# Half of the long-cache key products moved from VectorE to POOL, in place, in a two-layer hybrid decoder step

## What is computed

```python
def diff_attention(q, k, v, qpos, lam, lam_init):
    kpos = jnp.arange(k.shape[1], dtype=jnp.int32)
    def blk(qp, qb):
        s = jnp.einsum('bqhmd,bkhmd->bhmqk', qb, k) * (A_QK_DIM ** -0.5)
        p, _, _ = masked_softmax(s, kpos[None, :] <= qp[:, None])
        attn = p[:, :, 0] - lam * p[:, :, 1]
        return jnp.einsum('bhqk,bkhd->bqhd', attn.astype(v.dtype), v)
    o = blockwise(blk, qpos, q)
    return rmsnorm(o) * (1.0 - lam_init)
# for the samples: k = concatenate([cache_a_k[page_table], new key]), 1025 keys of 4 x 2 x 64
```

## Time and profile before

| | |
|---|---|
| median of 3 runs | 826.94 us (823.4 to 831.84) |
| the profiled execution | 828.67 us |
| its span, first to last instruction | 826.9 us |
| mean granted TensorE clock in it | 0.972 of full speed |

### The profile page before, as it was taken

The page is one execution under the profiler, slowest core; times in us unless marked ns, Lnnn a source line. Parts: engine busy times, 40 slices in busy tenths (PEclk is TensorE's granted clock), DMA queues, the critical chain, the costliest instruction groups (busy, mean ns, idle before and its releaser), DMA issues.

```text
span 826.9 us, 12677 instructions
## 1 busy us (share of the span) xinstructions
PE 755.6 (91%) x4874; PEld 404.9 (49%) x4874; DVE 426.0 (52%) x958; ACT 241.2 (29%) x601; POOL 164.6 (20%) x202
## 2 busy tenths in 40 slices
PE   6789999999898899999999998899899799999896
PEld 4456555444454334434454554555464455564543
DVE  2203598999968989645253243323654425421214
ACT  5324333222214101122254323333320233242222
POOL 0332412011330233430101022511131001001000
PEclk9999999999999799999999999999998999999899
DMA  8656668889896678796695394777779967856901
GB/s 287 206 203 220 242 244 320 309 307 376 281 321 209 228 245 299 229 340 247 218 321 183 126 405 166 282 265 273 262 248 386 377 252 284 304 173 258 356 1 54
DMA packets 67829, 213.08 MB, mean 258 GB/s; under 512 B 5056, under 2 KB 28785, under 8 KB 61881
## 3 DMA queue, kind: packets, MB, share of 16 engines
q0 software_dynamic: 20320, 142.55, 47.1%
q1 hardware_dynamic: 47288, 69.62, 24.0%
q10 hardware_dynamic: 160, 0.11, 0.0%
HBM read 206.22 MB, written 64.68 MB: 328 GB/s over the span
## 4 chain that ended last, share of the span: by engine, by line
PE 64%; DVE 17%; DMA 7%; ACT 5%; issue 5%; another core or an unknown queue 1%; POOL 0%; DVEq 0%; ACTq 0%; SPq 0%
PE psum L914 28%; PE psum L980 10%; PE psum L844 7%; PE psum L925 4%; DMA ring<-in_w_in_odd 4%; DVE SA L2334 3%; PE psum L1069 2%; DVE ring L2331 2%; PE psum L895 2%; DMA ring<-in_cache_a_v,index_a 2%; PE psum L1035 2%; PE psum L1320 2%; PE psum L1165 1%; ACT Z L1463 1%
## 5 line engine op out<-in xcount | busy, mean ns | idle before, releaser
L914 PE MATMUL psum<-ring,XB 128*128 128x512 f32 (+3 forms) x760 | 329.3, 587 | 4.1 <-DMA ring<-in_w_in_odd 3.3
L914 PEld LDWEIGHTS psum<-ring,XB 128*128 128x128 f32 x760 | 144.4, 195 | 161.3 <-issue 153.8
L980 PE MATMUL psum<-Z,ring 128*128 128x512 f32 x256 | 119.7, 613 | 2.1 <-issue 1.2
L1892 DVE TENSOR_TENSOR RT<-Z,const 128x128 f32<-128x128 f32 (+6 forms) x43 | 11.5, 267 | 145.1 <-ACT Z L1553 112.5
L980 PEld LDWEIGHTS psum<-Z,ring 128*128 128x128 f32 x256 | 47.2, 193 | 61.9 <-issue 60.8
L1553 ACT ACTIVATE Z<-psum,stat 128x512 f32<-128x512 f32 (+3 forms) x38 | 24.1, 635 | 179.6 <-PE psum L914 172.4
L925 PE MATMUL psum<-ring,XB 128*8 128x128 f32 (+3 forms) x1664 | 49.9, 267 | 4.7 <-issue 3.1
L925 PEld LDWEIGHTS psum<-ring,XB 128*8 128x8 f32 x1664 | 41.6, 89 | 23.0 <-issue 22.0
L1717 ACT ACTIVATE SM<-SM,stat 128x128 f32<-128x128 f32 (+4 forms) x56 | 26.9, 480 | 72.5 <-DVE stat L2081 71.4
L1463 ACT COPY NW<-psum 128x512 f32<-128x512 f32 (+1 forms) x56 | 32.7, 584 | 47.9 <-PE psum L844 41.6
L2164 DVE MAX8 small<-KC 8x8 f32<-8x1025 f32 x32 | 38.9, 1217 | 1.6
(11 more groups left out here) (347 smaller groups left out, 902.0 us busy)
## 6 DMA issues: line engine op xcount, KB each, us to landing
ring<-in_w_in_odd SPq DMA_DIRECT2D x9, 2048.0 KB, 13.2
ring<-in_w_in_even SPq DMA_DIRECT2D x6, 2048.0 KB
ring<-in_cmp_w SPq DMA_DIRECT2D x4, 2048.0 KB
ring<-in_w_in_odd SPq DMA_DIRECT2D x8, 1024.0 KB
out_s_d_k<-in_state_d_k POOLq DMA_DIRECT2D x8, 1022.0 KB
out_s_d_v<-in_state_d_v POOLq DMA_DIRECT2D x8, 1022.0 KB
Z<-in_cmp_w POOLq DMA_DIRECT2D x5, 1024.0 KB, 8.0
ring<-in_state_d_v POOLq DMA_DIRECT2D x5, 1024.0 KB, 7.6
```

Source lines behind the costliest of these rows:

```text
L914: last = mm(out[:, 0:n], xT[:, k, t * 128:(t + 1) * 128], w[:, k * n:(k + 1) * n], start=k == 0, stop=k == KT - 1)
L980: last = mm(out[:, h * 512:(h + 1) * 512], w[:, (r % 16) * CH + h * 128:(r % 16) * CH + h * 128 + 128], rowsT[:, at:at + 512], start=r == ...
```

## The change

For the second half of every entry (half = 1), the product with the query is computed by POOL, in place in the same buffer, and VectorE's `score_a(b, 1)` waits for the semaphore `multiplied` and then only sums. The first halves stay as they were. POOL's product stands in POOL's queue: before an item is issued, POOL multiplies the next entry b if the load `ak{b}_1` is already issued and if the step `score_a(b, 1)` comes at most `POOL_LEAD` = 14 steps of `ORDER` after the step that frees the item's buffer (an item whose former user is no load of POOL counts as free from the start, `default=-1`, and has no product put ahead of it).

```diff
+POOL_LEAD = 14
...
-                kv = ap(slot[:, 0:1], [512, 4], [1, 512])
-                tt(kv, kv, ap(queries[:, 0:1], [0, 4], [1, 512]), mul).then_inc(step, 1)
-                wait_own(step)
+                if half:
+                    eng.wait_ge(sem("multiplied"), b + 1)
+                else:
+                    kv = ap(slot[:, 0:1], [512, 4], [1, 512])
+                    tt(kv, kv, ap(queries[:, 0:1], [0, 4], [1, 512]), mul).then_inc(step, 1)
+                    wait_own(step)
...
+            def multiply(b):
+
+                name = f"ak{b}_1"
+                pool.wait_ge(*arrival[name])
+                if b == 0:
+                    pool.wait_ge(*marks["query_a"])
+                kv = ap(slot_of(name)[:, 0:1], [512, 4], [1, 512])
+                nc.gpsimd.tensor_tensor(kv, kv, ap(queries[:, 0:1], [0, 4], [1, 512]), ALU.mult)\
+                    .then_inc(sem("multiplied"), 1)
+
+
+            issued, multiplied = set(), 0
             for name, queue, parts in items:
                 if queue == "pool":
+                    freed = max([last_use[n] for n in place[name][1] if n in last_use], default=-1)
+                    while multiplied < NB and f"ak{multiplied}_1" in issued \
+                            and step_of["score_a", multiplied, 1] <= freed + POOL_LEAD:
+                        multiply(multiplied)
+                        multiplied += 1
+                    issued.add(name)
                     stream(pool, name, parts)
```

## The result

The changed kernel took a median of 843.81 us (841.71 to 853.13, four runs); the kernel before, on the same chip, 826.4 us (823.4 to 831.84, four runs). The ratio is 1.0225, with a 95% interval from 1.0132 to 1.0318. So the change costs 1.7 to 2.3%, 14 to 19 us by these ratios (17.4 and 12.3 us by the differences of the medians), where 8.0 us were forecast. The profiled executions are 841.71 us (span 839.9) after and 828.67 (span 826.9) before: 13.0 us, and those are the ones that the traces explain.

What follows compares the result with a forecast made beforehand. The prediction took TensorE as the bound, with VectorE's lateness costing at most some 4 us. Added waits of 2.8, 2.2 and 3.0 us summed to 8.0 us, giving a median of 834.9 us, range 825 to 843.

Steps and rivals of the forecast that it cites:

- The price of the multiply: One 128x2048 f32 multiply on POOL: taken as 4.57 us, the upper end, with 2.29 us as the lower.
- The exclusion: POOL's multiplies and VectorE's two-input operations hold each other up, while one-input reductions pass.
- M1 to M3 have room: POOL's multiplies for entries 1 to 3 (M plus entry number): VectorE gains 3 x 2.3 us less what they block.
- Rival 2: Multiplies of entries 1 to 6 each hold VectorE for all 4.57 us: 846.4 us, chance 16%.
- Step B: POOL's multiplies for entries 4 to 6 make VectorE late; 2.2 us reaches TensorE at 226.09 through the softmax.
- Step A: Entry 0's multiply holds a VectorE rope near 83 us, making TensorE's index queries 2.8 us late.
- M4: POOL's multiply for entry 4, queued behind ak6_0, runs 187.1 to 191.7; VectorE's reduction waits, 1.8 us late.
- M5: POOL's multiply for entry 5: waits for VectorE's L2331, runs 198.0 to 202.6, and makes L2055 wait 1.8 us.
- Step C: Entry 7's multiply, behind rows1_2 and four copies, delays TensorE's maxima by 3.0 us, counted from a TensorE event.
- the relief: VectorE loses 18.3 us of multiplies; TensorE's three idle pieces between 100 and 240 us return at most some 4 us.
- Rival 1: No exclusion between POOL and VectorE, multiply price 4.57 us: +1.6, 828.5 us, chance 20%.
- rival 3: A multiply of 2.29 us without exclusion, so VectorE runs ahead: -3.4, 823.5 us, chance 12%.

Runs made afterwards that it cites:

- The kernel with entries 0 to 2: POOL multiplies the second halves of entries 0 to 2 only, VectorE the others, against the kernel before: 814.79 us, ratio 1.0016.
- the second pair: The unaltered changed kernel measured again on another chip against the kernel before: 826.67 us against 814.38, ratio 1.0173.
- the kernel with entries 4 and 5: POOL multiplies the second halves of entries 4 and 5 only, VectorE the others, against the kernel before: 819.84 us, ratio 1.006.

## Why the prediction was wrong, step by step

**The price of the multiply** was right: 4.51 to 4.54 us against 4.57. The Trainium skill's 4.50 us (GPSIMD Engine Reference, Performance versus the Vector engine) is nearer still.

**The exclusion** was right for what it named and named too little. Two-input operations are held (2.94, 5.79 and 4.41 us for 0.29, 0.48 and 2.29). The step that failed is the sentence "M1 to M3 have room": it went through the queue and asked only for two-input operations in the way. M3 met the one-input L2030. Price: 5.1 us of stall and 1.8 us of slower turns behind it, 6.9 us, against nothing. Rival 2 had dismissed the same place with "M1 and M3 meet few of the others". Step B, below, is the other large error and of about the same size.

**Step A**, +2.8, measured 0 (1.0 us ahead at that point). The hold came as told, 2.94 us ending after M0. But TensorE's turn of the index queries began at 83.55, while the rope was held until 85.46, so it was not waiting for the rope. In the earlier trace rows the rope ended 0.48 us before that turn, and the trace named another releaser, which I overrode by nearness. The kernel with entries 0 to 2 bears it out: 8.4 us of holds, and TensorE's distance unchanged over them.

**Step B**, +2.2, measured +9.8 less the 3.4 regained. The wait for M4 came (3.95 us of idle time). The error is what M5 meets. Its readiness was as forecast, 1.8 us after the reduction (201.27 to 203.11). But I had it wait there for the next first-half product and then meet L2055, for 1.8 us, and took L2099 to be over by then. By the records it would have been: it begins at 202.14 and needs 0.48. What failed is the premise that a multiply holds nothing before it begins. L2099, on which TensorE's turn depends directly, was held from 0.97 us before M5's record to its end, 5.3 us more than its own length. M6 and L2335 went nearly as told (4.41 us, a hold of 2.1 against 3.2).

**Step C**, +3.0, measured +2.7; mechanism as written, M7 from 250.09, a wait of 8.12 us for the forecast 8, TensorE idle for 2.55 us. "Counted from a TensorE event" held.

**What was not in the sum.** First, the price of a stall beyond its length: 4.7 us (1.8 and 2.9) in slower turns behind the waits of 5.43 and 7.72 us; the granted clock was 0.50 from 170.0 to 172.6 us and 0.52 from 208 to 214. Second, the relief. "At most some 4 us" became 14 by the ratio, which is why the other two terms, 28 to 32 us by the same ratios, end at 14 to 19. Counting three idle pieces of one trace left out two of the same kind (0.67 and 1.38 us) and what the clock gave back behind them.

**The rivals.** Rival 2, 846.4 us by a hold for every multiply, is closest to the 843.81. That nearness is in part luck, since two of its terms were not right: A cost nothing, and the holds did not cost by their sum (18.0 us) but by the two that a turn of TensorE hung on. Rival 1 (no exclusion) and rival 3 (a short multiply) are excluded by the rows. The forecast's sign was right. Its range ended at 843, seven tenths of the way from 834.9 to rival 2 (the prediction says half way and further), and the first pair left it by 0.8 us; the second pair's 1.0173 would be 841.2 us on the 826.94, inside it. So the number was missed narrowly, because errors of both signs met: A and the relief on one side, entry 3, M5 and the clock on the other.

**What stays open.** L2099's hold begins at 202.14, 0.97 us before M5's record begins; this repeats at 182.62 against 183.62 in the kernel with entries 4 and 5. The load and the copy alone do not do it, as shown above; why the hold starts ahead of the multiply's record was not tested. The 3.6 us (16.6 to 13.0) that come back after 260 us go at least in part with the clock: 2.9 us come back at 778 to 787 us of the kernel before, where its granted clock is 0.52 on the mean, while the changed kernel does the same matmuls at 1.00 (790 to 811 us).

## What to carry to other kernels

Before work is moved to POOL, lay it against VectorE's instructions one by one and sort those by kind, not by number of inputs: reductions, MAX8 and MATCH_REPLACE8 passed beside a multiply, two-input operations and TENSOR_SCALAR on SBUF did not, and the cost is set by the one held operation that the bounding engine waits for. Leave a margin of 1 us ahead of the multiply's recorded start as well. Cut the piece to the length of an instruction that passes and start it by that instruction's predecessor: the same kind of multiply then gave 0.9913 where it had cost 1.02. If an engine has lost work and its busy time has not fallen, look for instructions of unusual length; that is how a hold looks in a profile.

## What the runs showed of the hardware that was not expected

- A fill by POOL, which reads nothing, held VectorE's TENSOR_SCALAR for its whole length (0.43 us became 3.86) and let two-input operations pass (0.29 and 2.29 us).
- POOL's multiply was never lengthened: the eight lie between 4.51 and 4.54 us, also where a two-input operation or TENSOR_SCALAR of VectorE had begun 0.07 to 0.97 us earlier. No run has a multiply that began when such an operation had been going for more than 1 us. A product on VectorE that met one took 4.41 us for 2.29.
- A hold can be longer than the multiply: 5.79 and 5.80 us beside 4.52 and 4.51, where the multiply was queued behind a load and a copy. The same load and copy without a multiply behind them held nothing (0.48 us).
- Matmuls after a stall of 5.43 us took 3.60 for 1.93 us, and after 7.72 us 6.25 for 3.60, with the granted clock in those stretches at 0.91 and 0.87 on the mean.
- Relief of a second engine gave back more than the first one's idle pieces: 14 us by the ratio and 9.6 between the profiles, where the marked pieces of the stretch that vanished came to 5.6.
